# Strassen's seven products for the first four k tiles of the gate and up blocks of a two-layer block kernel

## What is computed

```python
D_MODEL, SEQ, D_FF = 2048, 256, 5632
h = rms_norm(x, norm_ffn_pre[l])
f = (jax.nn.silu(h @ w_ffn_gate[l]) * (h @ w_ffn_up[l])) @ w_ffn_down[l]
x = x + rms_norm(f, norm_ffn_post[l])
```

## Time and profile before

| | |
|---|---|
| time, median of 3 runs | 2297.91 us (2297.87 to 2298.04) |
| the profiled execution's own time | 2298.06 us |
| its span | 2296.4 us |
| TensorE (PE) busy | 2285.4 us, 100% |
| VectorE (DVE) busy | 1443.3 us, 63% |
| ScalarE (ACT) busy | 1172.7 us, 51% |

### The profile page before, as it was taken

One profiled execution on the slowest core, in us unless ns is written; L12 is line 12 of the kernel. 1 busy time (PEld: TensorE's weight loads), 2 busy tenths in 40 slices (PEclk: granted clock), 3 DMA queues, 4 the chain that ended last, 5 costly groups with the idle time before them and its releaser, 6 DMA issues.

```text
span 2296.4 us, 27501 instructions
## 1 busy us (share of the span) xinstructions
PE 2285.4 (100%) x10741; PEld 1916.4 (83%) x10741; DVE 1443.3 (63%) x1902; ACT 1172.7 (51%) x1535; POOL 25.6 (1%) x35
## 2 busy tenths in 40 slices
PE   9999999999999999999999999999999999999998
PEld 7888888888888888888888888888888888888887
DVE  6677777756666645555455555675677756576864
ACT  6555655444445744444444444465555456556443
POOL 0000000000000000000000000000000000000000
PEclk9999999999999999999999999999999999999999
DMA  8566665766667566666666666656565665656553
GB/s 296 177 194 200 193 187 172 225 202 204 192 203 273 171 200 208 202 207 210 195 203 203 201 195 221 228 180 190 168 179 171 206 216 153 198 159 184 173 200 135
DMA packets 258578, 452.03 MB, mean 197 GB/s; under 512 B 23601, under 2 KB 63537, under 8 KB 257809
## 3 DMA queue, kind: packets, MB, share of 16 engines
q1 hardware_dynamic: 258016, 449.74, 62.7%
q10 hardware_dynamic: 432, 0.53, 0.1%
HBM read 434.99 MB, written 2.10 MB: 190 GB/s over the span
## 4 chain that ended last, share of the span: by engine, by line
PE 97%; DVE 2%; ACT 1%; DMA 0%; SPq 0%; issue 0%; DVEq 0%; ACTq 0%
PE pm L993 30%; PE pm L995 30%; PE pm L994 30%; PE pb L681 1%; PE pb L863 1%; DVE wl L2246 1%; PE pb L761 1%; PE pb L771 0%; DVE yR L1788 0%; DMA raw<-in_w_in 0%; ACT wh L1500 0%; PE pm L988 0%; PE pm L987 0%; PE pm L982 0%; PE pm L986 0%; PE pm L981 0%
## 5 line engine op out<-in xcount | busy, mean ns | idle before, releaser
L2246 DVE TENSOR_TENSOR wl<-raw,wh 128x1024 fp32r<-128x1024 f32 (+3 forms) x786 | 947.8, 1210 | 739.0 <-ACT wh L1500 736.7
L1500 ACT ACTIVATE wh<-raw 128x1024 fp32r<-128x1024 f32 (+3 forms) x786 | 819.2, 1046 | 899.7 <-PE pm L995 894.8
L993 PE MATMUL pm<-wh,hTh 128*128 128x512 f32 x702 | 275.2, 392 | 1.1 <-DVE wl L2246 1.1
L993 PE MATMUL pm<-wh,x2Th 128*128 128x512 f32 x704 | 273.9, 389 | 0.0
L994 PE MATMUL pm<-wl,x2Th 128*128 128x512 f32 x704 | 273.9, 389 | 0.0
L995 PE MATMUL pm<-wh,x2Tl 128*128 128x512 f32 x704 | 273.9, 389 | 0.0
L995 PE MATMUL pm<-wh,hTl 128*128 128x512 f32 x702 | 273.3, 389 | 0.0
L994 PE MATMUL pm<-wl,hTh 128*128 128x512 f32 x702 | 273.3, 389 | 0.0
L993 PE MATMUL pm<-wh,xT3h 128*128 128x512 f32 (+1 forms) x640 | 249.0, 389 | 0.0
L995 PE MATMUL pm<-wh,xT3l 128*128 128x512 f32 (+1 forms) x640 | 244.6, 382 | 0.0
L994 PE MATMUL pm<-wl,xT3h 128*128 128x512 f32 (+1 forms) x640 | 244.4, 382 | 0.0
(11 more groups left out here) (427 smaller groups left out, 3160.4 us busy)
## 6 DMA issues: line engine op xcount, KB each, us to landing
raw<-in_w_in SPq DMA_DIRECT2D x286, 512.0 KB, 3.7
raw<-in_w_ffn_gate SPq DMA_DIRECT2D x88, 512.0 KB, 4.3
raw<-in_w_ffn_up SPq DMA_DIRECT2D x88, 512.0 KB, 4.0
raw<-in_w_ffn_down SPq DMA_DIRECT2D x88, 512.0 KB, 4.1
raw<-in_w_o SPq DMA_DIRECT2D x64, 512.0 KB, 4.3
raw<-in_w_in SPq DMA_DIRECT2D x68, 256.0 KB, 3.3
raw<-in_w_branch_b SPq DMA_DIRECT2D x32, 512.0 KB, 3.9
raw<-in_w_out SPq DMA_DIRECT2D x32, 512.0 KB, 4.7
```

The costliest lines, as they stand in the source:

```text
L993: e.matmul(o, ah[:, kk, t], h[:, c], start=first, stop=False)
L1500: e.activation(h[:, 0:n], r[:, 0:n], ACT.Copy).then_inc(s["hi"], 1)
L2246: e.tensor_tensor(l[:, 0:n], r[:, 0:n], h[:, 0:n].bitcast(F32), ALU.subtract).then_inc(s["lo"], 1)
```

## The change

For c from 1 to 10 (ten of eleven blocks) the k tiles 0 to 3 of gate and up are taken together. The activations of these four tiles make a 2 x 2 block matrix (token halves by pairs of k tiles) and so do the weights (pairs of k tiles by gate and up). Strassen's method in Winograd's form needs seven products instead of eight. Each product is one new slab and one step, with 6 matmuls. A new group `fs{c}` with these seven stands ahead of `fg{c}` and `fu{c}`, which keep the tiles 4 to 15 (6 slabs each).

- The order of the seven is b11, b21, b22 (plain weight slabs), then t1, t3, t2, t4 (sums of weight slabs). The sums are made by DVE in the raw buffers, in place (`SUMS`, line 2422), behind the split of b11, b21, t1 and t3. Both are 128 x 1024.
- b21 and b22 begin the accumulators `pm` of gate and up, and t4 adds to gate's. b11, t1, t2, t3 have banks of their own, `pb4` to `pb7`.
- ACT copies `pb4` to `C11`. DVE adds four times (`gathered`), twice more when the gate block is complete and twice when the up block is (`joined`). Silu and the multiplication then read `C11` to `C22` instead of PSUM.
- The sums of activations (`sform`) are made once, during fg0 (`forms`, `forms_high`).
- The four raw slabs of `fs{c}` are kept until the last product that reads them; SP waits by a table (`freed`).

```diff
+FORMS = ("b11", "b21", "b22", "t1", "t3", "t2", "t4")
+BLOCK = {"b11": 0, "t1": 0, "t2": 0, "t3": 1, "b21": 2, "t4": 2, "b22": 3}
+SUMS = {"b11": ("t1", 0, 1, 0), "b21": ("t3", 1, 3, 1), "t1": ("t2", 0, 3, 0), "t3": ("t4", 2, 2, 0)}
...
         for c in range(c0, c0 + n):
-            add(f"fg{c}", "x2T", a["w_ffn_gate"][0], 512 * c, ev=("a", 2))
-            add(f"fu{c}", "x2T", a["w_ffn_up"][0], 512 * c)
+            if c:
+                seven(f"fs{c}", "x2T", w_g, w_u, 512 * c, range(4))
+            kts = range(4 if c else 0, 16)
+            add(f"fg{c}", "x2T", w_g, 512 * c, kts=kts, ev=("d" if c else "a", 2))
+            add(f"fu{c}", "x2T", w_u, 512 * c, kts=kts)
...
-                w.wait_ge(s["lo"], p.split[j - NRAW])
+                w.wait_ge(s["lo"], p.split[p.freed[j - NRAW]])
...
+            for k in range(2):
+                cols = slice(512 * k, 512 * k + 512)
+                e.matmul(out, lhs[0][k], h[:, cols], start=(k == 0), stop=False)
+                e.matmul(out, lhs[0][k], l[:, cols], start=False, stop=False)
+                ins = e.matmul(out, lhs[1][k], h[:, cols], start=False, stop=bool(b) and k == 1)
...
+        if g.pair:
+            if kts[0] in ("t1", "t2", "t3", "t4"):
+                w.wait_ge(s["sums"], 4 * int(g.name[2:]) - 4 + int("1324"[int(kts[0][1]) - 1]))
+            e.activation(h[:, :], r[:, :], ACT.Copy).then_inc(s["hi"], 1)
...
+    def gathered(c):
+
+        n = 4 * c - 4
+        yield p.end[f"fs{c}"]
+        w.wait_ge(s["mm"], p.first[f"fs{c}"] + 6)
+        w.wait_ge(s["q_c"], c)
+        w.wait_ge(s["f_s"], 2 * c - 2)
+        e.tensor_tensor(m.C12[:, :], m.C11[:, :], m.pb[6][:, :], ALU.add).then_inc(s["q_d"], 1)
+        w.wait_ge(s["q_d"], n + 1)
+        e.tensor_tensor(m.C21[:, :], m.C12[:, :], m.pb[7][:, :], ALU.add).then_inc(s["q_d"], 1)
+        e.tensor_tensor(m.C12[:, :], m.C12[:, :], m.pb[5][:, :], ALU.add).then_inc(s["q_d"], 1)
+        w.wait_ge(s["q_d"], n + 2)
+        e.tensor_tensor(m.C22[:, :], m.C21[:, :], m.pb[5][:, :], ALU.add).then_inc(s["q_d"], 1)
...
+            e.tensor_tensor(l[:, :], r[:, :], h[:, :].bitcast(F32), ALU.subtract).then_inc(s["lo"], 1)
+            if kts[0] in SUMS:
...
+                e.tensor_tensor(R[into], R[x], R[y], ALU.subtract).then_inc(s["sums"], 1)
```

More of the change, by code:

```diff
@@ L603, in sync_program @@
     step = 0
-    for j in range(NRAW, len(p.slabs)):
-        while p.ahead(step) < j - NRAW:
+    for j in range(NRAW, len(p.loads)):
+        while p.ahead(step) < p.freed[j - NRAW]:
             step += 1
@@ L932, in tensor_program @@
     n = 0
-    for i, g in enumerate(p.groups):
-        acc = m.pm[i % 2]
+    for g in p.groups:
+        if g.pair:
+            while due <= n:
+                due = next(bg, p.steps)
+            seven(g, n)
+            n += len(FORMS)
+            continue
+        acc = m.pm[p.acc[g.name]]
+        joined = g.name[:2] in ("fg", "fu") and g.kts[0]
         layer_of = int(g.name[2:3]) if g.act in ("xT3", "qlT", "kvT") and g.name[:2] != "uk" else 0
@@ L942, in tensor_program @@
             h, l = m.wh[p.slot[j]], m.wl[p.slot[j]]
-            if k == g.kts[0] and i >= 2:
-                before = p.groups[i - 2]
+            if k == g.kts[0] and g.name in p.before:
+                before = p.before[g.name]
                 w.wait_ge(s[f"ev_{before.ev[0]}"], p.evac[before.name])
@@ L992, in tensor_program @@
                     o = acc[:, half, 0:g.n]
-                    e.matmul(o, ah[:, kk, t], h[:, c], start=first, stop=False)
+                    begun = joined and (half == 0 or g.name[:2] == "fg")
+                    e.matmul(o, ah[:, kk, t], h[:, c], start=first and not begun, stop=False)
                     e.matmul(o, ah[:, kk, t], l[:, c], start=False, stop=False)
@@ L1069, in taken, with forms_high @@
                          ).then_inc(s["ev_a"], 1)
+    def forms_high():
+        yield p.first["fg0"] + 6
+        w.wait_ge(s["s_d"], 5)
+        e.activation(m.sform[0][:, :, :, :], m.sraw[:, :, :, :], ACT.Copy).then_inc(s["s_h"], 1)
     def out_squares(name, key, c):
-        acc = m.pm[p.groups.index(p.g[name]) % 2]
+        acc = m.pm[p.acc[name]]
         w.wait_ge(s["mm"], p.end[name])
@@ L1449, in background @@
             for c in range(c0, c0 + n):
-                yield p.end[f"fg{c}"]
+                if c:
+                    yield p.first[f"fs{c}"] + 2
+                    w.wait_ge(s["mm"], p.first[f"fs{c}"] + 1)
+                    e.activation(m.C11[:, :], m.pb[4][:, :], ACT.Copy).then_inc(s["q_c"], 1)
+                else:
+                    yield from forms_high()
+                yield p.end[f"fg{c}"] + (c > 0)
                 w.wait_ge(s["rstd"], RS["r0"])
@@ L1453, in background @@
                     w.wait_ge(s["f_t"], c - 1)
-                taken(0, f"fg{c}", m.FST[c % 2], ACT.Silu, "r0")
+                if c:
+                    w.wait_ge(s["ev_d"], p.evac[f"fg{c}"])
+                    for half, of in ((0, m.C11), (1, m.C21)):
+                        e.activation(m.FST[c % 2][:, half, :], of[:, :], ACT.Silu, scale=m.rs["r0"][:, half:half + 1]
+                                     ).then_inc(s["f_s"], 1)
+                else:
+                    taken(0, f"fg{c}", m.FST[c % 2], ACT.Silu, "r0")
                 for i in range(2):
```

173 lines of the change are left out of this document (144 added, 29 removed).

## The result

The changed kernel takes 2335.28 us (2333.04 to 2336.3, 4 runs), the kernel before 2297.89 in the same series: ratio 1.0161, 95% interval 1.0144 to 1.0179. It is slower by 37.4 us, where 19.8 were forecast, and its time lies above the stated range.

A forecast was written before the change was run, and what follows sets the result against it. TensorE was taken as the bound nearly everywhere. Saved matmuls -13.6, waits in the products +23.6, waits at the up's third slab +8.0 and carry-over +1.8 gave +19.8 us on 2298.06: 2318 us, range 2307 to 2330.

The forecast's parts named there:

- both places of the waits: TensorE waits for DVE's splits at t3 and t2 in the products, then at the up's third slab.
- The first wait: In the seven products, TensorE waits 1.97 us at t3 and 0.92 at t2; 23.6 us over ten blocks.
- The carry-over: After a block with the second wait, DVE reaches joined some 0.35 us later; five blocks, 1.8 us.
- SP's pace: In an unbroken queue behind t2's split, each load or transfer across costs SP 0.60 us to issue.
- The chain behind the landing: After the transfers across land, ACT's high parts, then DVE's low parts, gathered additions and splits delay the up's third slab.
- t + 3.98 and t + 8.24: Up's second and third slab, counted from the transfers' landing t, forecast 27.0; third at 35.2, wanted at 34.2.
- The last starts at 24.1, and lands 2.9 later, at 27.0: Issue and landing of the last of 16 transfers across, in us into the block; 2.9 is a median.
- The upper bound of 4.2: Longest landing of a transfer across; with it the third slab's wait would be 2.3 us instead of 1.0.
- called the bytes free: Listed at no cost: nine loads and 16 small transfers in 15 us, some 350 GB/s against 387 in the trace.
- second wait: At the up's third slab, 1.0 us in each of eight blocks that follow an up block: 8.0 us.
- More than forecast: Rival, 10 in 100: landing takes 4.2 us under the burst, or DVE's operations don't overlap; 2328 us.
- this rival: Clock rival, 6 in 100: granted clock falls to 1.2 GHz in the products' gaps, 2.7 us in ten blocks; 2345.

The follow-up runs named there:

- k3: k1 with ACT's high parts and DVE's low parts of the down activations due later, behind the splits of the up's second and third slab: 2310.2 us, ratio 1.0054.
- k4: k3 with the two multiplications and the transposes between blocks of products due at 5 and 6 steps, transfers across one step later: 2291.35 us, ratio 0.9972.
- k6: k3 without the four sums of weight slabs in each block and ACT's waits for them: 2291.12 us, ratio 0.9971.
- k1: The changed kernel with the copy to C11 and the four gathered additions queued ahead of the down activations' high and low parts: 2317.65 us, ratio 1.0087.
- k2: The changed kernel with SP's transfers across due two steps earlier: 2318.68 us, ratio 1.0091.
- k8: The changed kernel with the 16 transfers across issued four by four, in the first four of their eight steps: 2309.48 us, ratio 1.0051.
- k5: The changed kernel with six of each block's 16 loads fetching only the first of their two k tiles: 2325.15 us, ratio 1.0119.

## Why the prediction was wrong

**Right.** 60 matmuls fewer (10741 to 10681). The bound and both places of the waits. The first wait, step by step: t3 at 7.40 and t2 at 9.67 in the blocks without carry-over, against 7.41 and 9.69 by hand. The carry-over: 1.3 us against 1.8. k3, k4 and k6, worked out with the same distances, came within 1.2 us of 2309, 2292 and 2292. SP's pace of 0.60 us an issue: 24.0 against 24.1. The chain behind the landing: with 29.4 put in, its own formulas t + 3.98 and t + 8.24 give the up's second slab at 33.4 and the third at 37.6; measured 33.3 and 37.6.

**The step that failed** is "The last starts at 24.1, and lands 2.9 later, at 27.0". The 2.9 was the median of transfers across in a queue where the DMA engines were busy two thirds of the time, four small ones standing behind each load. Here the last two stand directly behind a load, in a burst that fills the engines, and the last is there 0.4 us after that load is: 3.6 to 6.0 us after its issue, 4.7 in the mean. Two things are in this. Only two small transfers stand behind that load, so that it was issued 1.2 us before the last and not 2.4 or more; and it takes 5.5 us in the mean instead of the 4.2 of its counterparts in the kernel before. The upper bound of 4.2 came from the same quiet trace and was no bound. The prediction held 350 GB/s asked against 387 seen, and called the bytes free. It did not say that the engines stand still for 9.4 us ahead of the burst. With the mean of t = 29.0 the formula gives a second wait of 3.0 us instead of 1.0. Measured are 23.8 us over eight blocks instead of 8.0: 15.8 of the 17.4 us by which the time lies above 2318. The products add another 0.8. k1, k2 and k8 each take 16.6 to 25.8 us off by changing only what stands behind the landing or when it comes.

**Smaller terms.** The first matmul behind a wait lasts 0.50 us, not 0.39, and the slab ends 0.11 later. There are 40 such restarts, and none was in the sum, but most cost nothing: where the next wait follows, DVE decides when it ends, and it only becomes shorter. Counted are the last of the products in ten blocks and the last of the second wait in eight, some 2 us. In blocks 2, 3, 4, 5 and 8 t1 starts 0.11 to 0.22 us late as well, which t3's wait takes up. From one b11 to the next block 2 takes 937.01 - 888.42 = 48.59 us. Without waits it would be 7 x 1.36 + 12 x 2.72 = 42.16. The difference of 6.4 is 3.2 in the products and 3.2 behind them, restarts included.

**Rivals.** "More than forecast" was the right one, by its first half (the landing under the burst), and too small. The clock did not move in the profile of the change: 1.00 in the stretch where TensorE is busy 7.32 of 9.40 us, so that this rival has no part in the miss there. But it is not an empty one: in k3's trace, with the same gaps, the clock fell once and cost 1.1 us. That is one swing of the kind that the Trainium skill describes (TensorE: Matmul & The Clock Gate, A second HAM failure mode: psum-queue depth-cycling), not the repeated one that the rival priced. DVE's operations overlap here too: the distance from t3's split to the sum behind it is 895.87 - 894.76 = 1.11 us, less than the split's 1.19, and by durations t2 would have been some 0.8 us late. The prediction put the Trainium skill's sentence (VectorE: DVE Perf Modes, The DRAIN you can't avoid) too strongly: the same paragraph ends by saying that a next operation which is not held starts earlier, and the starts in both traces are some 0.08 us earlier than that sentence alone would have them.

On the landing, the Trainium skill (DMA: Bandwidth & Descriptors, Queues, rings and completion order) says that a transfer's semaphore increment lands only after every earlier write from the same DMA engine. The last transfer fits that: 917.4 and 917.8, 915.0 and 915.5. The one before it, which lands at 916.5 ahead of the load, fits it only if it runs on engines that had finished their part of the load; no view here shows which it uses. I had not drawn on the rule.

**Left open.** Two runs shorten the load ahead of the last transfers from 5.5 us in the mean: k5 to 4.4, by fewer bytes with the same issues, and k8 to 4.1, with the same bytes and the loads further apart. Both fit a backlog of bytes in the engines; neither run shows the backlog itself. Why single blocks stay slow (5.3 in k5's block 2, 6.7 in block 8 of the change) was not separated. Nor was it measured how often the clock falls in executions that were not profiled; the four of the change differ by 3.3 us.

## What to carry to other kernels

A saving on the bounding engine that is paid on another is decided by the queue of the other in the stretch where the slabs get short, not by its average: here two multiplications and a transposition, put five steps later, turn +12 us (k3) into -6.6 (k4). When buffers are held longer, look at what the DMA queue does afterward: it stands idle, then sends everything at once, and a small transfer on which a chain hangs can be as late as the load ahead of it. Take its landing time from a full stretch of the trace, and keep what waits for it out of the way of the next splits.

## What was not expected of the hardware

Of two transfers of 32 KB issued right behind a load of 512 KB, the first landed up to 1.3 us before the load and the second 0.3 to 0.5 us after it, in a full queue (917.4 and 917.8) and in a thinner one (915.0 and 915.5). And a matmul that restarts TensorE behind a wait lasts 0.50 us instead of 0.39, so that a short wait costs more than it shows: the idle time in the trace, 0.17 us in which the matmul before it was still in the pipeline, and 0.11 unless another wait follows. With such waits close together the granted clock stayed at 1.00 in the blocks of the change, k1, k2, k5 and k8, and fell once, for 3.4 us, in k3.
